# HGRN decays as running products per block level, in a two-layer hybrid transformer trunk

## What is computed

```python
bcum = jnp.cumsum(lf_n, axis=2)          # log of the gates, summed over the chunk
b_last = bcum[:, :, -1]
s_next = s * jnp.exp(b_last)[..., None] + jnp.einsum(
    "bhcd,bhce->bhde", k_n * jnp.exp(b_last[:, :, None] - bcum), v_n)
dec = jnp.exp(jnp.where(incl[:, :, None], bcum[:, :, :, None, :] - bcum[:, :, None, :, :], -jnp.inf))
att = jnp.einsum("bhid,bhjd,bhijd->bhij", q_n, k_n, dec)
o = jnp.einsum("bhcd,bhde->bhce", q_n * jnp.exp(bcum), s) + jnp.einsum("bhij,bhje->bhie", att, v_n)
```

## Time and profile before

| | us |
|---|---|
| median of 3 runs | 3708.57 |
| lowest and highest run | 3698.99, 3709.93 |
| span of the profiled execution | 3711.6 |

### The profile page before, as it was taken

One profiled execution on the slowest core, in us unless ns is written; L12 is line 12 of the kernel. 1 busy time (PEld: TensorE's weight loads), 2 busy tenths in 40 slices (PEclk: granted clock), 3 DMA queues, 4 the chain that ended last, 5 costly groups with the idle time before them and its releaser, 6 DMA issues.

```text
span 3711.6 us, 38875 instructions
## 1 busy us (share of the span) xinstructions
PE 3250.4 (88%) x16792; PEld 2476.9 (67%) x16792; DVE 1523.6 (41%) x2008; ACT 1093.1 (29%) x1414; POOL 411.5 (11%) x262
## 2 busy tenths in 40 slices
PE   7977888899888898999999795978799678889998
PEld 3645848655666476888888464968756565558886
DVE  1334325212778253423432433515205973443444
ACT  3171211131323454312212334211222322552222
POOL 0000120200244010000000001030201441200000
PEclk9988999999988999999999887978899878999999
DMA  5111030121112101111212010000011000112231
GB/s 177 46 34 46 1 114 23 46 68 46 46 68 87 42 5 42 51 64 59 67 57 69 12 46 12 1 1 1 1 46 53 5 1 5 34 46 96 97 100 59
DMA packets 143360, 173.94 MB, mean 47 GB/s; under 512 B 5382, under 2 KB 116744, under 8 KB 143191
## 3 DMA queue, kind: packets, MB, share of 16 engines
q1 hardware_dynamic: 142240, 170.99, 13.8%
q0 software_dynamic: 672, 0.37, 0.1%
q10 hardware_dynamic: 279, 0.09, 0.0%
HBM read 169.35 MB, written 2.10 MB: 46 GB/s over the span
## 4 chain that ended last, share of the span: by engine, by line
PE 77%; DVE 12%; ACT 6%; issue 3%; POOL 2%; DMA 0%; DVEq 0%; SPq 0%; ACTq 0%
PE ps L889 24%; PE ps L482 18%; PE ps L525 4%; PE ps L632 4%; PE ps L649 3%; PE ps L868 3%; PE ps L652 3%; PE ps L502 2%; PE ps L830 1%; PE ps L819 1%; DVE region L1527 1%; PE ps L744 1%; DVE region L1500 1%; PE ps L758 1%; PE ps L665 1%
## 5 line engine op out<-in xcount | busy, mean ns | idle before, releaser
L482 PE MATMUL ps<-modulated,weights 128*128 128x512 f32 (+3 forms) x2080 | 695.2, 497 | 18.1 <-ACT modulated L992 11.3
L482 PEld LDWEIGHTS ps<-modulated,weights 128*128 128x128 f32 (+1 forms) x2080 | 398.5, 192 | 310.8 <-issue 280.4
L889 PE MATMUL ps<-region_r 128*128 128x512 f32 (+1 forms) x1536 | 382.0, 357 | 0.0
L889 PEld LDWEIGHTS ps<-region_r 128*128 128x128 f32 x1536 | 270.7, 188 | 44.1
L889 PE MATMUL ps<-modulated_r,region_r 128*128 128x512 f32 (+1 forms) x768 | 236.8, 363 | 20.6 <-DVE modulated_r L1621 20.4
L889 PE MATMUL ps<-mixed_r,region_r 128*128 128x512 f32 (+1 forms) x768 | 233.9, 359 | 0.0
L889 PE MATMUL ps<-mixed_r,weights_r 128*128 128x512 f32 (+1 forms) x768 | 231.0, 356 | 0.0
L889 PE MATMUL ps<-region_r,weights_r 128*128 128x512 f32 (+1 forms) x768 | 229.7, 354 | 0.0
L433 POOL TENSOR_TENSOR region<-region 128x1536 f32<-128x1536 f32 x44 | 147.2, 3351 | 608.5 <-DVE region L1487 389.9
L1284 DVE TENSOR_TENSOR weights_r<-weights,region_r 128x2048 fp32r<-128x2048 f32 x64 | 146.4, 2288 | 148.0 <-ACT region_r L970 148.0
L395 POOL TENSOR_TENSOR region<-k_f_sb,gdn_small 128x512 f32<-128x512 f32 x48 | 48.7, 1038 | 1327.8 <-ACT region L1086 1215.8
(11 more groups left out here) (298 smaller groups left out, 5182.4 us busy)
## 6 DMA issues: line engine op xcount, KB each, us to landing
weights<-in_w_mlp SPq DMA_DIRECT2D x64, 1024.0 KB, 5.2
weights<-in_w_ada SPq DMA_DIRECT2D x40, 1024.0 KB, 5.2
weights<-in_w_in SPq DMA_DIRECT2D x34, 1024.0 KB, 5.0
region<-in_w_ada SPq DMA_DIRECT2D x8, 1024.0 KB, 16.0
weights<-in_w_out SPq DMA_DIRECT2D x8, 1024.0 KB, 5.0
modulated<-in_x SPq DMA_DIRECT2D x1, 2048.0 KB, 15.0
out<-region SPq DMA_DIRECT2D x4, 512.0 KB, 2.7
weights<-in_w_in SPq DMA_DIRECT2D x2, 640.0 KB, 5.1
```

What stands on the lines that cost most here:

```text
L482: last = mm(dst[0:m, CTX + a:CTX + b], w[:, k, m0:m0 + m], rhs[:, k, a:b], start=(first and k == 0), stop=(final and k == ks - 1))
L889: last = mm(dst[:, CTX + a:CTX + b], w[:, k, m], r[:, a:b], start=(k == 0 and r is r_low), stop=(k == KB - 1 and w is low))
```

## The change

The gate is taken as a sigmoid on the way out of PSUM (HF), and lower bound and keys follow on VectorE. Exponential, reciprocal, logarithm and cumulative sums are gone, and with them the buffers, the exponentials of the pieces and all of GpSimd's work in the stage. Instead, `block_decays` multiplies the decays of neighbouring blocks, pairwise, into the decays of the next level, half as many each time; the last product is the decay of a whole chunk. `widen` multiplies, in place, the queries of one half of each block by the decay of the other half and the keys likewise, so that queries QF and keys HK are always decayed to the edge of the current block. There are now 21 steps per direction: seven levels by three pairs of chunks. In a step TensorE multiplies the keys of a chunk (128 columns of weights) by only those queries that lie in the receiving half, 64 columns for each of eight chunk and head pairs, which fill one PSUM bank; VectorE waits for the products, widens the pair, and makes one predicated copy of 512 elements. After the seven levels HK holds the keys decayed to the chunk's end; TensorE transposes them (24), and ScalarE instead of VectorE copies them out. QF is used in the scan as it is. The modulation halves stand one before each level, the eighth after the last level. The semaphores of the removed steps are gone too.

```diff
-        NLV = 9 * NC
+        NLEV, NPAIR = len(LEVELS), NC // 2
...
-        HK, HB = (blocks(2), blocks(4)), (blocks(3), blocks(5))
+        HK, HF, QF = (blocks(2), blocks(4)), (blocks(3), blocks(5)), (blocks(6), blocks(0))
         HATT = chunks(7)
-
-
...
-            return ap[:, :, 384 * (m % 2):384 * (m % 2) + 384]
+        PAIR_TOK = 256
+        def decays(d, lv):
+            if lv == 0:
+                return HF[d]
+            n = 4 * TOK // 2 ** lv
+            if lv == 1:
+                at = Y[:, 4:6, :].rearrange("p a b -> p (a b)")
+            else:
+                end = 4 * TOK - 24 - n
+                at = R[:, 3 if d == 0 else 5, end - n:end]
+            return at.rearrange("p (h n) -> p h n", h=H)
+        def halves(ap, lv):
+            return ap.rearrange("p h (n e s) -> p h n e s", e=2, s=2 ** lv)
+        def pair_of(ap, p):
+            return ap[:, :, PAIR_TOK * p:PAIR_TOK * (p + 1)]
...
-                pool.wait_ge(sq_used, number(SQUARES, l, "grms", 3) + 1)
-                for d in range(2):
...
-                    lvb = NLV * (2 * l + d)
-                    bank = 0
+                    mb, eb = NM * (2 * l + d), NEV * (2 * l + d)
                     if d == 1:
                         pe.wait_ge(ho_evac, o_count(l, 0, NC - 1))
                     pe.wait_ge(k_done, 2 * l + d + 1)
-                    for m in range(-2, 16):
-                        if m >= 0:
...
-                            bank += 1
+                    for ci in range(NC):
+                        cc = slice(128 * ci, 128 * ci + 128)
+                        for h in range(H):
+                            last = mm(ps[:, ci, 128 * h:128 * h + 128], HK[d][:, h, cc], HQ[:, h, cc], start=True, stop=True)
+                        last.then_inc(lv_out, 1)
+                    for i in range(NLEV * NPAIR):
+                        lv, p = divmod(i, NPAIR)
+                        if l == 0 and p == 0:
+                            ada_point(2 * ADA_GDN + 8 * d + lv, 2 * ADA_GDN)
+                        pe.wait_ge(m_ready, mb + i + 1)
+                        pe.wait_ge(lv_evac, eb + i + 1)
+                        q5 = halves(QF[d], lv)
+                        blocks_of = 64 // 2 ** lv
+                        for r in range(2 * H):
+                            ci, h = 2 * p + r // H, r % H
+                            last = mm(ps[:, i % 6, 64 * r:64 * r + 64].rearrange("p (n s) -> p n s", n=blocks_of),
+                                      HK[d][:, h, 128 * ci:128 * ci + 128], q5[:, h, blocks_of * ci:blocks_of * (ci + 1), 1 - d, :],
+                                      start=True, stop=True)
+                        last.then_inc(lv_out, 1)
+                    if l == 0:
+                        ada_point(2 * ADA_GDN + 8 * d + 7, 2 * ADA_GDN)
                     KE = chunks(3 if d == 0 else 5)
-                    pe.wait_ge(lv_evac, lvb + NLV)
+                    for ci in range(NC):
+                        if ci % 2 == 0:
+                            pe.wait_ge(m_ready, mb + NPAIR * NLEV + ci // 2 + 1)
+                        pe.wait_ge(lv_evac, eb + NPAIR * NLEV + ci + 1)
+                        for h in range(H):
+                            last = tr(ps[:, (NPAIR * NLEV + ci) % 6, 128 * h:128 * h + 128], HK[d][:, h, 128 * ci:128 * ci + 128], ident)
+                        last.then_inc(lv_out, 1)
+                    pe.wait_ge(lv_evac, eb + NEV)
+                    pe.wait_ge(ke_evac, NC * (2 * l + d) + NC)
...
-                                    mm(o, S[:, (n - 1) % 2, 64 * h:64 * h + 64], HK[d][:, h, 128 * ci:128 * ci + 128], start=True, stop=False)
+                                    mm(o, S[:, (n - 1) % 2, 64 * h:64 * h + 64], QF[d][:, h, 128 * ci:128 * ci + 128], start=True, stop=False)
...
-                for u in range(4):
-                    copied(l, "hf", u, af(HK[0][:, u, :], tokens(finished(l, "hf", u)), ACT.Copy))
...
-                af(HB[1], HK[1], ACT.Exp, bias=zero_col, scale=-1.0).then_inc(f_exp, 1)
+                for u in range(8):
+                    if u == 4:
+                        act.wait_ge(y_ready, 6 * l + 4)
+                    copied(l, "hf", u, af(HF[u // 4][:, u % 4, :], tokens(finished(l, "hf", u)), ACT.Sigmoid, bias=zero_col))
                 for ci in range(NC):
                     copied(l, "hi", ci, af(HV[:, ci, :], finished(l, "hi", ci)[:, 512:768], ACT.Copy))
                 for u in range(2):
                     copied(l, "hgate", u, af(HGT[:, u, lo:], tokens(finished(l, "hgate", u), lo), ACT.Silu, bias=zero_col))
-                act.wait_ge(k_done, 2 * l + 2)
-                af(HB[1], HB[1], ACT.Ln, bias=tiny_col).then_inc(lf_done, 1)
                 for d in range(2):
-                    for m in range(16):
-                        act.wait_ge(md_ready, 16 * (2 * l + d) + m + 1)
...
-                    af(HB[d], HB[d], ACT.Exp, bias=zero_col).then_inc(eb_ready, 1)
+                    if l == 0:
+                        for a in range(8):
+                            ada_point(2 * ADA_GDN + 8 * d + a, 2 * ADA_GDN)
+                    KE = chunks(3 if d == 0 else 5)
+                    for ci in range(NC):
+                        act.wait_ge(lv_out, NLV * (2 * l + d) + NEV + ci + 1)
+                        af(KE[:, ci], ps[:, (NPAIR * NLEV + ci) % 6, :].rearrange("p (h d) -> p h d", h=H), ACT.Copy).then_inc(ke_evac, 1)
...
-                    dve.wait_ge(f_exp, 2 * l + d + 1)
-                    link(v.tensor_scalar(HB[d], HB[d], 1.0, None, ALU.add))
-                    link(v.reciprocal(HB[d], HB[d]))
+                    dve.wait_ge(gemm_evac, number(UNITS, l, "hf", 4 * d + 3) + 1)
                     for h in range(H):
                         q = 4 * d + h
-                        last = v.tensor_scalar(HB[d][:, h, :], HB[d][:, h, :], lb[:, l, 1, q:q + 1], lb[:, l, 0, q:q + 1], ALU.mult, ALU.add)
+                        last = v.tensor_scalar(HF[d][:, h, :], HF[d][:, h, :], lb[:, l, 1, q:q + 1], lb[:, l, 0, q:q + 1], ALU.mult, ALU.add)
                     link(last)
-                    v.tensor_scalar(HK[d], HB[d], -1.0, 1.0, ALU.mult, ALU.add).then_inc(k_done, 1)
-                    dve.wait_ge(lf_done, 2 * l + d + 1)
...
-                queries_keys(0, 1)
+                    v.tensor_scalar(HK[d], HF[d], -1.0, 1.0, ALU.mult, ALU.add).then_inc(k_done, 1)
+                def block_decays(d, lv):
+                    src = decays(d, lv).rearrange("p h (n e) -> p h n e", e=2)
+                    dst = decays(d, lv + 1) if lv + 1 < NLEV else ebl[:, :, :]
+                    return v.tensor_tensor(dst, src[:, :, :, 0], src[:, :, :, 1], ALU.mult)
+                def widen(d, lv, p):
+                    n, s = PAIR_TOK // 2 ** (lv + 1), 2 ** lv
+                    q5, k5 = halves(pair_of(QF[d], p), lv), halves(pair_of(HK[d], p), lv)
+                    by = decays(d, lv).rearrange("p h (n e) -> p h n e", e=2)[:, :, n * p:n * (p + 1), :]
+                    q, k = 1 - d, d
+                    v.tensor_tensor(q5[:, :, :, q, :], q5[:, :, :, q, :], by[:, :, :, k].unsqueeze(3).to_broadcast([128, H, n, s]), ALU.mult)
+                    v.tensor_tensor(k5[:, :, :, k, :], k5[:, :, :, k, :], by[:, :, :, q].unsqueeze(3).to_broadcast([128, H, n, s]),
+                                    ALU.mult).then_inc(m_ready, 1)
                 for d in range(2):
-                    lvb = NLV * (2 * l + d)
-                    bank = 0
...
-                        queries_keys(1, 1)
+                    lvb, mb, eb = NLV * (2 * l + d), NM * (2 * l + d), NEV * (2 * l + d)
+                    for ci in range(NC):
+                        dve.wait_ge(lv_out, lvb + ci + 1)
+                        v.tensor_tensor(HATT[:, ci], ps[:, ci, :].rearrange("p (h d) -> p h d", h=H), over_heads(ident), ALU.mult).then_inc(lv_evac, 1)
+                        if ci % 2 == 1:
+                            v.tensor_tensor(pair_of(QF[d], ci // 2), pair_of(HQ, ci // 2), pair_of(HF[d], ci // 2), ALU.mult).then_inc(m_ready, 1)
+                    dve.wait_ge(lv_evac, eb + NC)
+                    for lv in range(NLEV):
+                        n, s = 64 // 2 ** lv, 2 ** lv
+                        dve.wait_ge(m_ready, mb + NPAIR * (lv + 1))
+                        link(block_decays(d, lv))
+                        for p in range(NPAIR):
+                            i = NPAIR * lv + p
+                            dve.wait_ge(lv_out, lvb + NC + i + 1)
+                            dve.wait_ge(m_ready, mb + i + 1)
+                            widen(d, lv, p)
+                            if lv:
+                                dve.wait_ge(lv_evac, eb + NC + i - NPAIR + 1)
+                            at = HATT[:, 2 * p:2 * p + 2].rearrange("p c h d -> p (c h) d").rearrange("p r (n e s) -> p r n e s", e=2, s=s)
+                            mask = masks[:, lv + (7 if d == 0 else 0), :].rearrange("p (n e s) -> p n e s", e=2, s=s)[:, :, 1 - d, :]
```

(24 more changed lines are left out.)

85 lines of the change are left out of this document (3 added, 82 removed).

## The result

The changed kernel takes 3618.45 us (median of 4 runs, 3616.76 to 3619.37) against 3704.24 us (4 runs, 3698.99 to 3709.93): a ratio of 0.977, 95% interval 0.9756 to 0.9784. It is faster by 86 us. The forecast was 3589 us, 119.5 us less; the time lies within the range, 29.5 us above the forecast. The profiled span went from 3711.6 to 3617.3 us.

The account below looks back on a forecast made before the run. Levels were taken as bound by a ring of four engines waiting on three buffers, scans by TensorE's half clock. Layer 0's 58.2 plus layer 1's 61.3 made 119.5 us off, 3589 from the median; range 3543 to 3640.

Parts of the forecast that it names:

- TensorE's records: Level products: same number of records, 64 columns no cheaper than 128; 0.115 us each at full clock, 0.214 at half.
- VectorE's work: Levels: 512-element product 0.60 us, copy 0.65 us, so 1.85 us a step and 7.3 to 5.75 us a level.
- rival 3: VectorE's strided forms cost up to twice, 3.3 us a step: near 3620 us; chance 0.13 together with dearer strided reads.
- the 2.4 us of cover: Layer 0 levels: VectorE stays hidden under TensorE's 9.07 us a level up to about 2.4 us a step.
- Layer 0: HGRN stage of layer 0 at full clock: levels 78.6 and 78.0, scans 21.6; 178.2 us against 236.4, 58.2 less.
- Layer 1's levels: Clock falls to half at the gap of 1.0 us after the second decay product; 74.0 us forward, 73.2 backward.
- the 16-column row: Trace row before the change: 16-column records start at full clock and fall to half though TensorE never pauses; cited against rival 1.
- Layer 1's scans: Both scans of layer 1 start at full clock behind the transposes: 9.4 and 8.7 us.
- Rival 1: Full clock through layer 1's levels too, VectorE pacing: 51.3 us a direction instead of 73.2, 3545 us in all; chance 0.20.
- Rival 2: Scans stay at half clock as before, since a gap precedes them: 35.5 us more, 3625 us; chance 0.09.
- Rival 4: TensorE at half clock through the levels of both layers: 77 us more, 3786 us, slower; chance 0.04.
- Rival 5: Stage's ring of waits replaced by another of the same length, so the time is the old one; chance 0.02.

Follow-up runs that it names:

- the extra product: Changed kernel with one more 128x512 product on VectorE in each of its 84 level steps, the step waiting for it: 3612.72 us, ratio 0.9732.
- full columns: Changed kernel with every level product streaming all 128 query columns instead of 64, same number of records: 3576.02 us, ratio 0.9648; in a later series 3570.57 us.
- the two first experiments: Changed kernel with all 128 query columns per level product: 3576.02 us; changed kernel with two unused 512-column products ahead of each layer 1 level: 3575.86 us.

## Why the prediction was right and wrong

- **TensorE's records.** Right: 64 columns in strided reads cost what 128 do, 5.47 us for 48 at full clock, 0.21 us each at half. Halving the columns saved nothing, as the sum had it, and the strided reads cost nothing.
- **VectorE's work.** The products were right (0.60 us from one to the next), the stage's strides cost them nothing. The copies at levels 0 and 1 were mis-sized, 1.28 instead of 0.65 us, so a step of 2.3. That was rival 3 for one operand at two of seven levels. It cost nothing, because it stayed under the 2.4 us of cover that the prediction named. That cover was larger than named: as the extra product shows, even 3.05 us at these two levels costs layer 0 nothing.
- **Layer 0.** Right: 78.1 + 77.5 for the levels (forecast 78.6 and 78.0), 23.4 for the scans (21.6), 179.0 in all against 178.2.
- **Layer 1's levels.** The term that was most off. The fall was right, its moment wasn't, and its reason only in part. "Where VectorE leaves gaps of about 1 us between them I take a fall", at the second decay product, after six steps. It came 13.3 us after the first product (15.0 backward), not after 17 to 18. In the forward direction three steps were done at full clock and 18 took 60.6 us, where I had seven at full clock and 14 at 3.42. That is 78.0 and 77.4 us for 74.0 and 73.2: 8 us. Gaps can't be the whole reason: with full columns a gap of 2.1 us ahead of these steps cost 1.7 us of clock in one direction and nothing in the other, and here TensorE was at half clock for 58.6 us with no gaps at all. But the fall did come 1.5 us behind one of 0.89 us, and in the backward direction 0.9 us behind one of 0.33. The other half of that paragraph, which held the 16-column row (half clock without a pause) against full clock, pointed the right way, as the two first experiments show for these records.
- **Layer 1's scans.** The first was right (9.9 us for 9.4). The second was 14.6 for 8.7: the clock rose only at 2997.4, behind the transposes, and fell again at 3000.8. That is 6 us: the scan did start at full clock, as "so I take it that the scans start at full" has it, but the sum set nothing aside for a fall inside it. That the clock rises behind the transposes was right both times (0.50 until 2907.5 and 1.00 from 2909.0, with nothing but transposes on TensorE between 2906.1 and 2910.2). The Trainium skill, "TensorE: Matmul & The Clock Gate", "Part 4: PE-mode transpose", says that transposes don't engage the full clock; the trace disagrees.
- **The rest.** The stage gave 104.1 us for 119.5. Another 9.8 us went outside it, where I had taken nothing; most of that is of the size of scatter. And the profiled execution before was slow beside its runs: 3711.6 us of span for a median of 3704.24, so 94.3 us of spans are 86 of medians. A sum against a profiled span should have kept that in mind. So all the large errors lie on the same side, none offset another, and about half of the 29.5 us (9.8 outside the stage, 4.3 from the profiled execution) is nothing that the prediction weighed.
- **The rivals.** Rival 1, full clock in layer 1, didn't come: TensorE was busy 58.58 of 58.60 us at 0.50. By the rule of the Trainium skill cited with it (an engine kept busy without long gaps) that stretch would be at 1.00; the trace disagrees. Had it held, the kernel with full columns, which VectorE paces at full clock, says 56 to 57 us a direction, not the 51.3 I gave it. Rival 2 came true for one scan of four. Rival 4, half clock through the levels, came true for most of layer 1 and not for layer 0, where the clock stood at 1.00 with the 512-column products among the steps. Rival 5 didn't come: TensorE waits 2.1 us for VectorE in layer 1's levels, where it waited 43.7.

## What to carry over

TensorE in fp32 costs per record, not per column, up to 128 columns here (0.115 us at full clock for 64 and for 128), so halving the streamed columns saves it nothing and can cost it the clock: when a stretch of narrow records stands at half clock, give it back its full columns or mix wide records in, even useless ones. Read the clock column beside the busy column: 100% busy at 0.50 is a stretch with up to half its time to win. Here 21 of 78 us were won, until VectorE set the pace, and by another mix of TensorE's records; faster copies on VectorE won nothing. And cut the work of other engines for the waits it ends: here 579 us of it were worth 94.

## What the hardware showed that I hadn't expected

- Two dummy products of 512 columns ahead of 24 narrow ones make the level shorter: 1.88 + 5.57 us at full clock instead of 10.2 at half.
- A predicated copy of 128x512 from PSUM takes 0.70 us when its target runs are four elements or longer, and 1.28 us when they are one or two; the stride of its mask makes no difference (1.29), and 1024 elements side by side take the same 1.28.
- A VectorE product beside GpSimd's subtraction of 1.89 us takes 2.07 us instead of 0.69: 1.38 us longer, nearly all of the 1.52 us that the two overlap.
- The same sequence of TensorE's records with the same gap of 1.04 us keeps the full clock in the profile of one kernel and loses it in that of another (0.45 and 0.70 us for four records).
- Behind a gap of 2.12 us, 128-column records fell to half clock for some 3 us and came back while they ran; 64-column records, once at half, stayed there for 58.6 us.
